# Hybrid decoder block: attention logits as three fp32r products instead of fp32, and a reciprocal root computed one slot later

## What is computed

```
h   = RMSNorm(x);  P = h @ W_in
yA  = GatedDeltaNet(P_A) * silu(z)        # 8 heads, chunked delta rule in stages
q   = rmsnorm(q_in) * q_norm_w            # 8 heads of 128
ks, kw = rmsnorm(...) * k_norm_w          # keys, selected and window branch, 2 groups
ls  = q . ks * scale + bias ; lw = q . kw * scale + bias
o   = g0 * softmax(lc) @ vc + g1 * softmax(ls) @ vs + g2 * softmax(lw) @ vw
x  += W_out(sigmoid(gA) * (yA @ W_pa) + sigmoid(gB) * (o @ W_pb))
x  += SwiGLU(RMSNorm(x))
```

## Time and profile before

| | us |
|---|---|
| median of 3 runs | 559.23 (557.43 to 561.15) |
| profiled execution | 559.03 |
| its span | 557.2 |
| PE busy / DVE / ACT / POOL | 547.5 / 396.8 / 305.0 / 69.7 |

### The profile page before, as it was taken

How to read it: one execution, slowest core, us unless ns; L and a number is a source line. 1 busy time by engine, 2 the same in 40 slices (tenths; PEclk the granted TensorE clock), 3 DMA queues, 4 the chain that set the end, 5 groups by cost and what they waited for, 6 DMA issues and landing times.

```text
span 557.2 us, 9253 instructions
## 1 busy us (share of the span) xinstructions
PE 547.5 (98%) x3583; PEld 472.6 (85%) x3583; DVE 396.8 (71%) x649; ACT 305.0 (55%) x528; POOL 69.7 (13%) x107
## 2 busy tenths in 40 slices
PE   8999999999999999999999999999999999999996
PEld 8999999877777897788888888988888888888884
DVE  6879879976578737998886557567665766665763
ACT  6767669436445646656565343655545454545450
POOL 4221211683410000052000000000000000000000
PEclk9999999999999999999999999999999999999999
DMA  9945766455995352253544465755665766665622
GB/s 302 257 150 165 248 197 227 154 188 177 254 273 183 122 195 75 87 179 115 154 149 150 162 213 163 200 171 152 184 193 173 205 182 196 190 188 170 208 76 76
DMA packets 95467, 98.97 MB, mean 178 GB/s; under 512 B 5125, under 2 KB 75688, under 8 KB 95296
## 3 DMA queue, kind: packets, MB, share of 16 engines
q1 hardware_dynamic: 93168, 94.68, 55.1%
q0 software_dynamic: 1968, 2.64, 2.4%
q10 hardware_dynamic: 288, 1.05, 0.6%
HBM read 96.67 MB, written 1.84 MB: 177 GB/s over the span
## 4 chain that ended last, share of the span: by engine, by line
PE 85%; DVE 10%; ACT 2%; issue 2%; DMA 1%; DVEq 0%; ACTq 0%
PE ps L1596 17%; PE ps L1598 17%; PE ps L1597 17%; PE ps L1710 14%; PE ps L1713 7%; PE ps L1815 4%; DVE w_lo L1058 3%; PE ps L1601 3%; PE ps L1685 1%; PE ps L1975 1%; ACT w_hi L668 1%; DVE sc L1387 1%; DVE s_nm L1388 1%; PE ps L1950 1%; PE ps L1832 1%
## 5 line engine op out<-in xcount | busy, mean ns | idle before, releaser
L1058 DVE TENSOR_TENSOR w_lo<-raw,w_hi 128x2048 fp32r<-128x2048 f32 x74 | 170.6, 2306 | 99.0 <-ACT w_hi L668 98.9
L668 ACT ACTIVATE w_hi<-raw 128x2048 fp32r<-128x2048 f32 x74 | 141.5, 1913 | 73.5 <-PE ps L1598 64.9
L1710 PE MATMUL ps<-h_both,w_hi 128*128 128x512 f32 x352 | 122.7, 397 | 0.3 <-issue 0.2
L1713 PE MATMUL ps<-h_both,w_lo 128*128 128x256 f32 x352 | 91.2, 280 | 0.3 <-DVE h_both L1084 0.3
L1710 PEld LDWEIGHTS ps<-h_both,w_hi 128*128 128x128 f32 x352 | 63.8, 188 | 14.1 <-issue 1.5
L1713 PEld LDWEIGHTS ps<-h_both,w_lo 128*128 128x128 f32 x352 | 66.4, 189 | 4.0 <-issue 0.6
L1596 PE MATMUL ps<-w_hi,h_both 128*128 128x512 f32 x160 | 65.3, 408 | 0.1
L1598 PE MATMUL ps<-w_hi,h_both 128*128 128x512 f32 x160 | 62.6, 391 | 0.0
L1597 PE MATMUL ps<-w_lo,h_both 128*128 128x512 f32 x160 | 62.5, 391 | 0.0
L1596 PE MATMUL ps<-h_both,w_hi 128*128 128x256 f32 x208 | 59.5, 286 | 0.0
L1598 PE MATMUL ps<-h_both,w_lo 128*128 128x256 f32 x208 | 58.8, 283 | 0.0
(11 more groups left out here) (383 smaller groups left out, 950.2 us busy)
## 6 DMA issues: line engine op xcount, KB each, us to landing
raw<-in_w_in SPq DMA_DIRECT2D x29, 1024.0 KB, 5.2
raw<-in_w_gate SPq DMA_DIRECT2D x22, 512.0 KB, 4.0
raw<-in_w_up SPq DMA_DIRECT2D x22, 512.0 KB, 5.3
raw<-in_w_down SPq DMA_DIRECT2D x11, 1024.0 KB, 4.9
raw<-in_cmp_w SPq DMA_DIRECT2D x8, 1024.0 KB, 6.6
raw<-in_w_proj_a SPq DMA_DIRECT2D x4, 1024.0 KB, 5.1
raw<-in_w_proj_b SPq DMA_DIRECT2D x4, 1024.0 KB, 5.0
raw<-in_w_out SPq DMA_DIRECT2D x4, 1024.0 KB, 5.1
```

Source lines behind the costliest of these rows:

```text
L668: nc.scalar.activation(w_hi[s % NSPL][:], raw[RAW_OF[n]][:], ACT.Copy).then_inc(hi_done, 1)
L1058: nc.vector.tensor_tensor(w_lo[s % NSPL][:], raw[RAW_OF[n]][:], w_hi[s % NSPL][:].bitcast(f32), ALU.subtract).then_inc(lo_done, 1)
L1710: cross = lambda stop: pe.matmul(banks[part][:], hi[:, k, part * P:(part + 1) * P], h_both[:, :, k, :], start=(k == 0), stop=stop)
L1713: end = pe.matmul(banks[part][:, 0:SEQ], lo[:, k, part * P:(part + 1) * P], h_hi[:, k, :], start=False, stop=False)
```

## The change

The keys of both branches move into one tensor `keysT` (group, branch, token). After the last use of `DTb` and `qT` ACT makes high parts in fp32r: `k_hi` (128x1024) and `q_hi` (two instructions of 128x1024), at the end of the first half of slot gz1. DVE makes the low parts `k_lo` and `q_lo` (three subtractions of 128x1024, written over `keysT` and `nqT`) in the second half of slot gz1, after o1 and the hidden layer. A unit's logits are then `three` products (high x high, high x low, low x high) of the queries with the keys of both branches at once, 2 x 128 or 2 x 256 columns. Besides, the ten operations of the queries' root move on DVE from slot cmpv1 to slot wv1, where they stand behind stage Y5 and the second turn of the inverse (1247).

```diff
--- before.py
+++ after.py
@@ -186,6 +186,7 @@
 MISC_SLOTS = {W2_K: (AT["sv", 1], 0), TURN_KC: (AT["wv", 0], 0), TURN_KS: (AT["wv", 1], 0), LOGITS_C: (AT["cmpv", 1], 1),
               TURN_KW: (AT["gz", 1], 0), TURN_LC: (AT["wv", 1], 1), TURN_PC: (AT["gz", 0], 1), W2_V: (AT["gz", 2], 0), ALL_OC: (AT["gz", 2], 1)}
 SOFTMAX_C, SOFTMAX_C_END = (AT["cmpv", 2], 0), (AT["gz", 0], 0)
+LOGIT_OPERANDS, LOGIT_LOWS = (AT["gz", 1], 0), (AT["gz", 1], 1)
 
 
 TURN_O = {(AT["mga", 2], 1): [0], (AT["mga", 3], 0): [1], (AT["mga", 3], 1): [2], (AT["pa", 0], 0): [3]}
@@ -288,9 +289,13 @@
         sub_m = at("sub_m", z_at + 5 * KB, [P, SUB * SUB])
         sub_t = at("sub_t", z_at + 6 * KB, [P, SUB * SUB])
         sub_tt = at("sub_tt", z_at + 7 * KB, [P, SUB * SUB])
-        nqT = own("nqT", [P, HEADS, SEQ])
+        nqT_at = take(8 * KB)
+        nqT, q_lo = at("nqT", nqT_at, [P, HEADS, SEQ]), at("q_lo", nqT_at, [P, HEADS, SEQ], f32r)
+        q_hi = ar(8, "q_hi", (P, HEADS, SEQ), f32r)
         bias_g = own("bias_g", [P, HEADS, SEQ])
-        ksT, kwT = own("ksT", [P, GROUPS, SEQ]), own("kwT", [P, GROUPS, SEQ])
+        keysT_at = take(4 * KB)
+        keysT, k_lo = at("keysT", keysT_at, [P, GROUPS, 2, SEQ]), at("k_lo", keysT_at, [P, GROUPS, 2, SEQ], f32r)
+        k_hi = ar(1, "k_hi", (P, GROUPS, 2, SEQ), f32r, off=2 * KB)
         vs, vw = own("vs", [P, TT, GROUPS, DH]), own("vw", [P, TT, GROUPS, DH])
         sc_at = take(4 * KB)
         sc = [at(f"sc{i}", sc_at + i * 2 * KB, [P, 2, SEQ]) for i in range(2)]
@@ -384,6 +389,7 @@
         stage_cols, flat_zero = sem("stage_cols"), sem("flat_zero")
         fac_ready, oc_added, oc_out = sem("fac_ready"), sem("oc_added"), sem("oc_out")
         cmp2_in = sem("cmp2_in")
+        k_hi_done, k_lo_done, q_hi_done, q_lo_done = (sem(n) for n in ("k_hi_done", "k_lo_done", "q_hi_done", "q_lo_done"))
         of_ready, zt, zs_done = sem("of_ready"), sem("zt"), sem("zs_done")
         nq_sq, nq_turned, nq_out = sem("nq_sq"), sem("nq_turned"), sem("nq_out")
         key_copied, key_in, key_n = sem("key_copied"), sem("key_in"), sem("key_n")
@@ -889,7 +895,7 @@
                 if m in (TURN_KS, TURN_KW):
                     act.wait_ge(m_pe, m + 1)
                     j = 0 if m == TURN_KS else 1
-                    dst = (ksT, kwT)[j][:].rearrange("p g (t c) -> p t g c", t=TT)
+                    dst = keysT[:, :, j, :].rearrange("p g (t c) -> p t g c", t=TT)
                     nc.scalar.activation(dst, log_ps[:].rearrange("p (t g c) -> p t g c", t=TT, g=GROUPS), ACT.Copy,
                                          scale=wk[:, 1 + j:2 + j]).then_inc(m_out, 1)
                 elif m == TURN_KC:
@@ -918,6 +924,14 @@
                 elif m == TURN_PC:
                     act.wait_ge(m_pe, m + 1)
                     nc.scalar.activation(pcT[:], log_ps[:].rearrange("p (a c) -> p a c", a=2 * TT), ACT.Copy).then_inc(m_out, 1)
+
+            def logit_operands():
+                act.wait_ge(g_mm, stage_use("v1", NB - 1) + 1)
+                act.wait_ge(m_out, TURN_KW + 1)
+                nc.scalar.activation(k_hi[:], keysT[:], ACT.Copy).then_inc(k_hi_done, 1)
+                act.wait_ge(nq_out, 4)
+                for p in range(2):
+                    nc.scalar.activation(q_hi[:, 4 * p:4 * p + 4, :], nqT[:, 4 * p:4 * p + 4, :], ACT.Copy).then_inc(q_hi_done, 1)
 
             def hidden(c):
 
@@ -1020,6 +1034,8 @@
                                              scale=zw[:]).then_inc(ya_hi_done, 1)
                     if half == 1 and n in TAIL:
                         split_hi(n + 2)
+                    if (n, half) == LOGIT_OPERANDS:
+                        logit_operands()
                     for i in slot_units(n, half):
                         unit(i)
                 if n == AT["pa", 0]:
@@ -1346,6 +1362,17 @@
                                                      bias_g[:, a:HEADS:2, first:first + CMP_STRIDE * (k - 1) + 1:CMP_STRIDE], ALU.add))
                     link(nc.vector.tensor_reduce(pcm[:], valid, AX.X, ALU.max))
                     nc.vector.tensor_tensor(valid, valid, pcm[:].unsqueeze(3).to_broadcast([P, 2 * TT, 4, NCMP]), ALU.subtract).then_inc(pc_s, 1)
+
+            def logit_operands():
+                dve.wait_ge(k_hi_done, 1)
+                dve.wait_ge(m_out, TURN_KW + 1)
+                nc.vector.tensor_tensor(k_lo[:], keysT[:], k_hi[:].bitcast(f32), ALU.subtract).then_inc(k_lo_done, 1)
+                dve.wait_ge(m_pe, LOGITS_C + 1)
+                dve.wait_ge(nq_out, 4)
+                for p in range(2):
+                    dve.wait_ge(q_hi_done, p + 1)
+                    nc.vector.tensor_tensor(q_lo[:, 4 * p:4 * p + 4, :], nqT[:, 4 * p:4 * p + 4, :], q_hi[:, 4 * p:4 * p + 4, :].bitcast(f32),
+                                            ALU.subtract).then_inc(q_lo_done, 1)
 
             def copy_oc():
                 dve.wait_ge(m_pe, ALL_OC + 1)
@@ -1542,7 +1569,7 @@
                     if half == 1 and n - 1 in (AT["cmpk", 3], AT["cmpv", 3]):
                         hidden(0 if n - 1 == AT["cmpk", 3] else 1)
                     if half == 0:
-                        if n == AT["cmpv", 1]:
+                        if n == AT["wv", 1]:
                             f = lambda n: col[n][:].rearrange("p h t -> p (h t)")
                             dve.wait_ge(nq_sq, 16)
                             link(radicand(f("t1"), f("rn"), 1.0 / DH, EPS))
@@ -1561,6 +1588,8 @@
                         nc.vector.scalar_tensor_tensor(ya_lo[:, 2 * b:2 * b + 2, :].rearrange("p k c -> p (k c)"), gdn_ps[stage_use("ot", b) % GRING][:], zw[:],
                                                        ya_hi[:, 2 * b:2 * b + 2, :].rearrange("p k c -> p (k c)").bitcast(f32),
                                                        ALU.mult, ALU.subtract).then_inc(ya_lo_done, 1)
+                    if (n, half) == LOGIT_LOWS:
+                        logit_operands()
                     if (n, half) == (AT["gz", 2], 1):
                         copy_oc()
                     for i in slot_units(n, half):
@@ -1946,9 +1975,11 @@
                         pe.wait_ge(s_done, i)
                     else:
                         pe.wait_ge(m_out, TURN_KW + 1)
-                    for a, keys in enumerate((ksT, kwT)):
-                        last = pe.matmul(log_ps[:, a * SEQ:a * SEQ + w], nqT[:, h, t * P:(t + 1) * P], keys[:, h // 4, 0:w], start=True, stop=True)
-                    last.then_inc(l_mm, 1)
+                        pe.wait_ge(k_lo_done, 1)
+                    if h % 4 == 0 and t == 0:
+                        pe.wait_ge(q_lo_done, h // 4 + 1)
+                    three(((q_hi, q_lo), (k_hi, k_lo)), log_ps[:].rearrange("p (a c) -> p a c", a=2)[:, :, 0:w],
+                          lambda q: q[:, h, t * P:(t + 1) * P], lambda k: k[:, h // 4, :, 0:w], True, True).then_inc(l_mm, 1)
                 if 2 <= i < len(UNITS) + 2:
                     j = i - 2
                     h, t = UNITS[j]
```

## The result

The changed kernel takes 562.61 us (median of 14 executions, 561.68 to 565.74), the kernel before 559.28 us (14 executions, 557.43 to 561.15). The ratio is 1.0067, with an interval of 1.0050 to 1.0083: slower by 0.7%, with 1 outside the interval. A second comparison on another chip gave 1.0093 (1.0057 to 1.0129). The forecast was 564.3 us, or 0.9%.

A forecast was written before the change was run, and what follows sets the result against it. PE bounds the kernel (85% of the chain), except where DVE has no gap, 219.87 to 260.50 us. Copies +5.75, root -0.28, logits -0.34 give +5.13 on 559.03, 564.16, median 564.3 us; range 560.8 to 567.5.

The forecast's parts named there:

- ACT copies and the first stall: Slot gz1: three ACT copies put the tanh 3.07 us later, so PE's fourth o1 block is 2.6 us late.
- DVE copies and the second stall: Ahead of the second zs evacuation: gz2's second half starts 5.75 us late, 3.15 of it from DVE's copies.
- three take 3.55: DVE's three low-part subtractions ahead of the second zs evacuation take 3.55 us together (3.4 to 3.7).
- The root: Moved behind Y5: frees 0.72 us of PE idle, but delays gz0's split, so 0.28 us stay (0 to 0.72).
- The logits: Attention units: 2.1 us of PE work saved, only 0.34 cashed, at two chain logits (266.07, 284.50); DVE limits the rest.
- Rival 2: PE's clock halves in one of two idle stretches, doubling gz2's second-half products: +2.8 us, 567.1; chance 0.12.
- A granted clock under 1.00: Sign of being wrong: PE's clock in the changed trace below the full 1.00 that the sum assumes.
- Rival 1: Attention units: PE's logits saving of 2.1 us cashed in full, root 0.72; +2.9 us, 562.2; chance 0.20.
- rival 4: Not slower: zs reads are not PE's last wait, copies hidden, only gains of 0.6 to 2.8 us; about 558; chance 0.08.
- Rival 3: Late gz3 split frees its buffer late, SP's next load delays a split in DVE's full stretch: up to 1.5 us, 565.8; chance 0.10.
- The sum: Whole kernel: +5.75 - 0.28 - 0.34 = +5.13 us on the profiled 559.03, so 564.16; median 564.3, +0.9%; chance 0.50.

The follow-up runs named there:

- Numbers 5 and 6: 5: changed kernel, ACT's copies behind the tanh of gz1's first bank, ratio 1.0103; 6: changed kernel, DVE's subtractions one half slot later, 562.09 us, ratio 1.0078.
- number 8: Changed kernel with 11 filler fp32 matmuls ahead of o1's fourth block and 12 ahead of gz2's second half; 561.75 us, ratio 1.0072.
- Number 3: Changed kernel with all copies kept, but logits again as two fp32 matmuls, made of the low parts alone; 563.43 us, ratio 1.0094.
- number 4: Changed kernel with twelve filler fp32 matmuls only ahead of gz2's second half; 563.41 us, ratio 1.0086.
- number 7: Changed kernel with the same six copies spread over idle time, q_hi in two halves of own storage; 557.09 us against 557.64, ratio 0.9988.
- number 10: Changed kernel again without an edit, beside the kernel before on the same chip; 562.95 us against 558.15, ratio 1.0093.

## Why the prediction was right, and where its terms were off

**ACT copies and the first stall** (tanh 3.07 us late, PE 2.6). Right in path, releaser and size: the tanh is 3.05 us late once the 0.30 us by which everything runs early is taken off. Reckoned from the first o1 matmul (207.15 against 207.46), the fourth o1 block (210.97 against 208.79) is 2.49 us late.

**DVE copies and the second stall** (gz2's second half 5.75 us late, 3.15 of it here). Right in kind, a little too large: reckoned from o1 in the same way it is 5.39 us late (10.63 us behind o1's start against 5.24), 2.90 of it here. The term mis-sized is "three take 3.55": from 213.64 to 217.05 they took 3.41, since each overlaps the next by 0.08, and the first began 0.09 before the end of the operation ahead of it, which the forecast had counted end to start. That these copies add to the first stall instead of hiding in it was forecast. Numbers 5 and 6 confirm it from both sides: with either block moved alone most of the loss stays, since the other block, or the stretch that DVE limits, takes over.

**The root** (0.28 of 0.72 forecast; 0.25 in the changed kernel, 0.23 alone, nothing when undone). Right, with the split as the next thing late.

**The logits** (0.34 of 2.1 forecast; 0.26 in the profile, 0.32 with a steady clock). Right in size and in the main reason: the stretch of 68 DVE instructions has the same busy time as before and is 0.05 us shorter. But the places are in part others, and that the size fits so well is in part luck. The forecast took 0.17 at each of two logits on the chain, at 266.07 and 284.50, and nothing in the DVE stretch. In number 8 the shift falls from 5.42 to 5.28 by the split at 255.49, stays there to 282.36, and is 5.09 at 291.13: 0.14 within DVE's stretch, nothing at 266, 0.19 at the second place. Number 3, with the old logits, shows neither step.

**Rival 2, the clock** (chance 0.12, +2.8 us). A granted clock under 1.00 was named as a sign of being wrong, and ten of 14 executions of the changed kernel have one, so the sum stood although its premise of a steady clock did not: that is luck in part. The size was right, 2.67 us, of which 2.45 in the twelve products that it named. The error was to treat the two idle stretches alike. The fall comes after either in different executions. Behind the first stall it is paid out of the wait for zs, all of it or all but 0.3 us (number 4); only behind the second is it paid in full. By span and mean clock that happened in 2 of 14 executions, so the median does not hold it, while the profiled execution does. Its evidence, rows 11, was weak: one filler of 34 took 581 ns, and the profile gives a granted clock of 1.00 in each of those first microseconds. The Trainium skill (TensorE: Matmul & The Clock Gate, "Why this matters for your kernels") advises against idle gaps between bursts of matmuls; the traces agree: the clock fell behind idle stretches of 2.3 to 3.3 us in some executions, and number 8, where the gaps are filled, shows no fall in four.

**Rival 1** is refuted by number 3 and **rival 4**, for this placement, by every row. That a placement exists where it holds is shown by number 7. **Rival 3** left no trace: behind mga0 the splits keep their shift in number 8, less what the logits give back, and DVE is as busy in the full stretch as before, so no split waits there for a late load.

**The sum.** The usual span rose from 555.5 to 560.1. The terms from number 8's trace are 5.36 - 0.25 - 0.32 = 4.79, against the forecast's 5.13; less the 0.35 us slip in before's feed-forward part, 4.4. The forecast's 0.34 too much is almost all in the copies, 5.75 against 5.36 to 5.39. What remains lies in the base line. The forecast took the profiled execution of 559.03 us as ordinary; its output transfers were 1.5 us longer than the changed kernel's, and an execution with a span of 557.2 is like the slower fifth of before's. The medians say +3.3 us in the first comparison and +4.8 in the second (562.95 less 558.15). Their intervals, 2.8 to 4.6 and 3.2 to 7.2 us, overlap; a rise of 5.1 lies above the first and inside the second. In the first comparison the kernel before was slower than elsewhere: ten of its 14 executions took over 559.1 us, and three of the 35 beside the experiments did. Their spans are not on record, so whether these had the long end is not shown. The measured 562.61 lies in the range forecast, 560.8 to 567.5, and within 1%.

Still open: what makes the output transfers take 4.2 to 4.5 us in some executions, where the 0.35 us around 462 us come from, and why the clock falls in some executions and not in others.

## What to carry to other kernels

Before counting what PE saves, look at which engine has no gap in the stretch where the saving falls: 2.1 us were worth 0.3 here. Work for an engine with a fixed order belongs *ahead* of a wait it makes anyway; the same six copies cost 5.4 us behind the wait and nothing in front of it or between evacuations that nobody needs at once. If new idle stretches of PE can't be avoided, ask of each what follows: here a half clock ahead of another wait cost 0 to 0.3 us, one ahead of dense products that set the pace 2.7.

## What was not expected of the hardware

- The clock fell after idle times of 2.3 to 3.3 us of PE, but with the same instructions in the same order it did so in some executions only, and at three different places: behind the first stall (0.66 in the stretch from 210 to 215 us of number 3), inside the products behind it (number 10), behind the second stall (0.69 and 0.63). With one stall of 3.28 us it fell in four of four, by their mean clocks.
- Removing a stall made the kernel no faster, and slower than number 8 on the same chip (1.0103 against 1.0072): with two stalls eight of 14 executions have the mean clock of a fall at the harmless place, four no fall and two the costly one; with one stall all four have the costly one.
- The five output transfers at the end took 4.18 and 4.51 us in the two profiled executions of the kernel before, and 2.68 or 2.69 in the ten of all other kernels. That is 1.5 to 1.8 us, about as much as separates the usual spans of before (555.1 to 555.8) from the longer ones.
